# A fused two-block model on one core: the forgetting row in two parts, gates through a scratch row, c as one row, recurrence steps between tiles, one FFN product moved

## What is computed

```python
# first_block
mod = silu(c) @ w_ada + b_ada                    # c: 2048, w_ada: 2048 x 12288
sh1, sc1, gt1, sh2, sc2, gt2 = split(mod, 6)     # gt1, gt2: the two gates, rows of 2048
h = rmsnorm(x, g_mix) * (1 + sc1) + sh1
x = x + gt1 * hybrid_mixer(h, ...)
h = rmsnorm(x, g_ffn) * (1 + sc2) + sh2
x = x + gt2 * ((silu(dwconv(h @ w_gate)) * (h @ w_up)) @ w_down)

# forgetting attention, in the mixer, 8 heads
F = cumsum(log_sigmoid(f_logit + b_f))
s = q @ k.T * scale + F[t] - F[s]                # causal, softmax, @ v

# recurrence, in the mixer
log_a = -8 * gate_r * softplus(-lam);  a = exp(log_a)
inp = sqrt(-expm1(2 * log_a)) * (gate_i * xc)
h = scan(h = a * h + inp);   y_lru = h * gelu(yb)

# second block, twice; its last step
x = x + merged @ w_out
```

## Time and profile before

| | |
|---|---|
| median of 3 runs | 3060.62 us (3060.08 to 3062.21) |
| the profiled execution, its time | 3060.53 us |
| its span | 3058.7 us |
| granted TensorE clock, mean | 0.998 |
| busy: TensorE / its weight loads | 3026.9 us (99%) / 2543.3 (83%) |
| busy: DVE / ACT / POOL | 1973.8 (65%) / 1502.3 (49%) / 13.0 |
| read from HBM | 655 MB, 215 GB/s over the span |

### The profile page before, as it was taken

The page is one execution under the profiler, slowest core; times in us unless marked ns, Lnnn a source line. Parts: engine busy times, 40 slices in busy tenths (PEclk is TensorE's granted clock), DMA queues, the critical chain, the costliest instruction groups (busy, mean ns, idle before and its releaser), DMA issues.

```text
span 3058.7 us, 38978 instructions
## 1 busy us (share of the span) xinstructions
PE 3026.9 (99%) x14626; PEld 2543.3 (83%) x14626; DVE 1973.8 (65%) x2077; ACT 1502.3 (49%) x1804; POOL 13.0 (0%) x28
## 2 busy tenths in 40 slices
PE   7999999999999999999999999999999999999999
PEld 6899888888888888888888888888888888888887
DVE  7988887875666567675555656565475555556564
ACT  5555456544444445554444344544555454444543
POOL 0000000000000000000000000000000000000000
PEclk9999999999999999999999999999999999999999
DMA  9997887865555555455555445555455555445455
GB/s 400 416 383 290 338 343 278 315 244 193 190 186 190 188 185 179 165 179 179 193 172 193 166 170 193 173 186 186 160 183 175 194 175 194 166 167 193 168 183 191
DMA packets 167622, 659.24 MB, mean 216 GB/s; under 512 B 18592, under 2 KB 18880, under 8 KB 155200
## 3 DMA queue, kind: packets, MB, share of 16 engines
q1 hardware_dynamic: 164256, 637.99, 59.3%
q0 software_dynamic: 3232, 19.36, 1.7%
HBM read 655.18 MB, written 2.10 MB: 215 GB/s over the span
## 4 chain that ended last, share of the span: by engine, by line
PE 94%; DVE 4%; DMA 1%; ACT 1%; issue 0%; ACTq 0%
PE pg L1175 27%; PE pg L1177 27%; PE pg L1176 27%; PE pm L1210 1%; DVE R L1746 1%; PE pm L1238 1%; DMA w_raw<-w 1%; DVE w_lo L1802 1%; PE pm L1633 1%; PE pg L1264 1%; PE pg L1266 1%; PE pg L1265 1%; PE pm L1175 1%; PE pm L1177 1%; PE pm L1176 1%; PE pm L1527 0%
## 5 line engine op out<-in xcount | busy, mean ns | idle before, releaser
L1682 DVE TENSOR_TENSOR w_lo<-w_raw,w_hi 128x1024 fp32r<-128x1024 f32 x872 | 1066.0, 1225 | 961.3 <-ACT w_hi L607 957.2
L607 ACT ACTIVATE w_hi<-w_raw 128x1024 fp32r<-128x1024 f32 x872 | 925.0, 1061 | 1306.2 <-PE pg L1177 1299.2
L1175 PE MATMUL pg<-w_hi,hT_hi 128*128 128x512 f32 x2912 | 1146.7, 394 | 15.8 <-DVE w_lo L1802 15.5
L1177 PE MATMUL pg<-w_hi,hT_lo 128*128 128x512 f32 x2912 | 1135.4, 390 | 0.0
L1176 PE MATMUL pg<-w_lo,hT_hi 128*128 128x512 f32 x2912 | 1135.0, 390 | 0.0
L1175 PEld LDWEIGHTS pg<-w_hi,hT_hi 128*128 128x128 f32 x2912 | 547.8, 188 | 131.6 <-issue 14.5
L1177 PEld LDWEIGHTS pg<-w_hi,hT_lo 128*128 128x128 f32 x2912 | 547.4, 188 | 115.3
L1176 PEld LDWEIGHTS pg<-w_lo,hT_hi 128*128 128x128 f32 x2912 | 547.9, 188 | 110.0
L1175 PE MATMUL pg<-w_hi,y_parts 128*128 128x512 f32 x864 | 337.9, 391 | 2.3 <-issue 1.4
L1177 PE MATMUL pg<-w_hi,y_parts 128*128 128x512 f32 x864 | 336.4, 389 | 0.0
L1176 PE MATMUL pg<-w_lo,y_parts 128*128 128x512 f32 x864 | 336.2, 389 | 0.0
(11 more groups left out here) (302 smaller groups left out, 1953.5 us busy)
## 6 DMA issues: line engine op xcount, KB each, us to landing
w_raw<-w SPq DMA_DIRECT2D x1012, 512.0 KB, 4.1
R<-w_ada SPq DMA_DIRECT2D x59, 1024.0 KB, 9.2
x_rows<-w_ada SPq DMA_DIRECT2D x18, 1024.0 KB, 8.8
R<-w_ada POOLq DMA_DIRECT2D x11, 1024.0 KB, 7.7
R<-w SPq DMA_DIRECT2D x16, 512.0 KB, 11.2
R<-w_ada SPq DMA_DIRECT2D x10, 512.0 KB, 6.4
R<-mem_T SPq DMA_DIRECT2D x8, 512.0 KB, 10.0
x_rows<-x SPq DMA_DIRECT2D x4, 1024.0 KB, 14.8
```

What stands on the lines that cost most here:

```text
L607: act.activation(w_hi[:, g % RING, :, :].rearrange("p c n -> p (c n)"), raw[:, g % RING, :], ACT.Copy).then_inc(hi_done, 1)
L1175: pe.matmul(out, hi, w_hi[:, slot, c, :], start=start, stop=False)
L1177: return pe.matmul(out, lo, w_hi[:, slot, c, :], start=False, stop=stop)
L1682: tt(flat(w_lo[:, g % RING, :, :]), raw[:, g % RING, :], flat(w_hi[:, g % RING, :, :]).bitcast(F32), ALU.subtract).then_inc(lo_done, 1)
```

## The change

- **c.** SP loads c as one row, and `con`'s first part, ahead of everything. TensorE spreads the row over the partitions with four fp32 products of `ones` (one partition) with 512 columns, into four banks, ahead of tile 0. ACT applies SiLU as it evicts them, behind memory part 0 and tiles 0 and 1.
- **F.** A new tile `F_parts` in fp32r holds the rounded row in partitions 0 to 7 and the rest in 32 to 39; `F_pick` has ones in both places of a head. One fp32r product takes the place of the fp32 one. DVE makes both behind the scan, a memset is added.
- **Gates.** `gate_row` transposes 16 columns of `mod` into 16 rows on TensorE, ACT copies them to SBUF, POOL stores the 8 KB to a scratch row in HBM, waits for it, and loads it spread over 128 partitions (1 MB). Gate 1 in POOL's program stands ahead of the blocks of w_ada and behind the second attention; gate 2 behind these blocks and ahead of the late constants.
- **Recurrence.** On ACT tile 70 moves ahead of Tanh, the copy of F_t and tile 71 ahead of Square, tile 72 ahead of Identity; DVE's two products get a finer wait and one moves behind tile 73.
- **FFN.** In turns 0 and 1 `weigh_odd(5)` moves behind `down_out` 0 and 1. In the end the last product moves ahead of one tile.
- **End.** No tiles of zeros; the last 512 columns are added and stored in two halves.

```diff
         F_row = mv[:, 1, 1, 0:S]
+        F_parts = mv_r[:, 1, 1, S:2 * S]
+        F_pick = small_r[:, 0:NH * 2]
+        gate_rows = [mv[0:KD, 1, 0, 0:P], con[0:KD, 2 * P:3 * P]]
+        gates = [nc.dram_tensor(f"gate_rows{h}", (1, D), F32, kind="Internal").ap() for h in range(2)]
...
                 if g == 0:
+                    sp.dma_start(flat(c_rows)[0:1, :], t["c"].partition_broadcast(1)).then_inc(c_in, 16)
+                    sp.dma_start(con[:, 0:2 * P], t["con"][:, 0:2 * P]).then_inc(con_in, 16)
                     memory(0)
...
                     sp.dma_start(vec[:, :], t["vec"]).then_inc(vec_in, 16)
-                    sp.dma_start(con[:, 0:2 * P], t["con"][:, 0:2 * P]).then_inc(con_in, 16)
                 if g in (1, 3, 5):
                     memory((g + 1) // 2)
-                if g == 2:
-                    sp.dma_start(flat(c_rows), t["c"].partition_broadcast(P)).then_inc(c_in, 16)
...
                 tiles(group)
-            tiles(GROUPS, count=RING)
-            for n in range(NB):
+            for n in range(NB - 1):
                 sp.wait_ge(xb_ready, LAYERS * NB + n + 1)
...
                              ).then_inc(out_stored, 16)
-            sp.wait_ge(out_stored, 16 * NB)
+            for tb in range(TB):
+                sp.wait_ge(out_half, tb + 1)
+                sp.dma_start(t["out"][:, tb, (NB - 1) * NW:], x[:, tb, (NB - 1) * NW:]).then_inc(out_stored, 16)
+            sp.wait_ge(out_stored, 16 * (NB - 1 + TB))
...
             pool.dma_start(band, t["band"]).then_inc(band_in, 16)
+            def gate(h, dest):
+                pool.wait_ge(gate_sb, h + 1)
+                pool.dma_start(gates[h].rearrange("o (m p) -> (o m) p", p=P), gate_rows[h]).then_inc(gate_out, 16)
+                pool.wait_ge(gate_out, 16 * (h + 1))
+                pool.dma_start(dest, gates[h].partition_broadcast(P)).then_inc(gate_in, 16)
+            pool.wait_ge(y_ready, 2)
+            pool.wait_ge(lru_dve, 4)
+            gate(0, gate_1)
             for n in range(BY_SP, len(BLOCKS)):
...
                                    t["w_ada"][n][:, first:last]).then_inc(ffn_ada_in[at], 16)
-            pool.wait_ge(y_ready, 2)
+            gate(1, gate_b)
...
-            def broadcast(h, dest, bank):
-                act.wait_ge(bc_ready, h + 1)
-                at = (h % 2) * AH
-                for n in range(2):
-                    act.activation(dest[:, at + n * NW:at + (n + 1) * NW],
-                                   pm[bank + n][:, :], ACT.Copy).then_inc(bc_done, 1)
+            def gate_row(h):
+                act.wait_ge(gate_T, h + 1)
+                act.activation(gate_rows[h], pm[0][0:KD, 0:P], ACT.Copy).then_inc(gate_sb, 1)
...
                 upto(2 * p + 2)
-                if p == 1:
-                    act.wait_ge(c_in, 16)
-                    act.activation(flat(c_rows), flat(c_rows), ACT.Silu).then_inc(c_ready, 1)
+                if p == 0:
+                    for n in range(NB):
+                        act.wait_ge(c_ps, n + 1)
+                        i = act.activation(flat(c_rows)[:, n * NW:(n + 1) * NW], pm[n][:, :], ACT.Silu)
+                    i.then_inc(c_ready, 1)
...
             i.then_inc(lru_act, 1)
+            upto(71)
             for b in range(4):
...
             i.then_inc(lru_act, 1)
-            act.wait_ge(lru_act, 4)
-            act.activation(flat(GR), flat(Y_), ACT.Square).then_inc(lru_act, 1)
-            act.wait_ge(lru_act, 5)
-            act.activation(flat(GR), flat(GR), ACT.Identity, bias=1.0, scale=0.044715).then_inc(lru_act, 1)
             upto(72)
...
             act.activation(flat(F_t), pm[2][:, 0:TB * 8], ACT.Copy, scale=-1.0).then_inc(F_sb, 1)
+            act.wait_ge(lru_act, 4)
+            act.activation(flat(GR), flat(Y_), ACT.Square).then_inc(lru_act, 1)
+            upto(73)
+            act.wait_ge(lru_act, 5)
+            act.activation(flat(GR), flat(GR), ACT.Identity, bias=1.0, scale=0.044715).then_inc(lru_act, 1)
...
             take(g0 + 1, 1, flat(u_tok))
-            broadcast(2, gate_b, 0)
-            broadcast(3, gate_b, 2)
+            act.wait_ge(y_ready, 2)
+            gate_row(1)
...
-            def broadcast(h, bank):
-                first = (M_GATE1, M_GATE1 + 8, M_GATE2, M_GATE2 + 8)[h]
-                pe.wait_ge(ada_used, first + 8)
-                for m in range(8):
-                    i = pe.matmul(pm[bank + m // 4][:, m % 4 * P:(m % 4 + 1) * P],
-                                  mod[:, first + m:first + m + 1].to_broadcast([P, P]), ident, start=True, stop=True)
-                i.then_inc(bc_ready, 1)
+            def gate_row(h):
+                first = (M_GATE1, M_GATE2)[h]
+                pe.wait_ge(ada_used, first + KD)
+                pe.transpose(pm[0][0:KD, 0:P], mod[:, first:first + KD], ident).then_inc(gate_T, 1)
...
                         pe.matmul(out, Q1[occ][:, h, tb * P:(tb + 1) * P], K1[occ][:, h, :], start=True, stop=False)
-                        i = pe.matmul(out, ident[:, forget + h:forget + h + 1].to_broadcast([P, P]), F_row,
+                        i = pe.matmul(out, F_pick[:, forget + h:forget + h + 1].to_broadcast([P, P]), F_parts,
...
+            pe.wait_ge(c_in, 16)
+            pe.wait_ge(con_in, 16)
+            for n in range(NB):
+                pe.matmul(pm[n][:, :], ones[0:1, :], flat(c_rows)[0:1, n * NW:(n + 1) * NW], start=True, stop=True
+                          ).then_inc(c_ps, 1)
             upto(12)
             pe.wait_ge(rows_ready, 1)
-            pe.wait_ge(con_in, 16)
+            pe.wait_ge(c_ready, 1)
...
             pe.wait_ge(F_sb, 1)
+            pe.wait_ge(F_split, 1)
             attn_at(71, 0, Zv[0], "k0", 0)
...
             upto(86)
-            broadcast(0, 0)
+            gate_row(0)
             upto(91)
             pe.wait_ge(y_T_sb, 2)
-            pe.wait_ge(bc_done, 2)
+            pe.wait_ge(gate_sb, 1)
             attn_at(91, 1, Zv[1], "k1", 4)
...
             y_T(1, o1)
-            upto(106)
-            broadcast(1, 0)
...
             pe.wait_ge(aT_ready, j + 1)
-            broadcast(2, 0)
-            broadcast(3, 2)
+            gate_row(1)
             for n in range(NB):
...
                 if n == 0:
-                    pe.wait_ge(bc_done, 8)
+                    pe.wait_ge(gate_sb, 2)
...
                                    ).then_inc(F_ready, 1)
+            dve.wait_ge(F_ready, 1)
+            step(dve.tensor_copy(F_parts[0:8, :], F_row[0:8, :]))
+            step(tt(F_pick, ident[:, 0:8], ident[:, 32:40], ALU.add))
+            step.settle()
+            tt(F_parts[32:40, :], F_row[0:8, :], F_parts[0:8, :].bitcast(F32), ALU.subtract).then_inc(F_split, 1)
...
             step.settle()
-            dve.wait_ge(lru_act, 4)
+            dve.wait_ge(lru_act, 3)
             step(tt(flat(X_), flat(A_), flat(A_), ALU.mult))
...
             upto(73)
+            dve.wait_ge(lru_act, 4)
             stt(flat(TH), flat(X_), 1.0, flat(TH), ALU.add, ALU.mult).then_inc(lru_dve, 1)
+            upto(74)
...
                     split(g0 + 2, (i,))
-                    weigh_odd(i)
+                    if i < 5:
+                        weigh_odd(i)
                 down_out(g0 + 2, j, 0)
...
                 down_out(g0 + 2, j, 1)
+                weigh_odd(5)
...
             down_out(g0 + 2, j, 1)
-            split(g0 + 3, range(2))
-            dve.wait_ge(bc_done, 8)
+            split(g0 + 3, range(1))
             product(NFF - 1, aT2_hi, aT2_lo)
+            split(g0 + 3, range(1, 2))
...
                     dve.wait_ge(tile_used, tile0 + use.end)
+                    if l == LAYERS - 1 and use.n == NB - 1:
+                        for tb in range(TB):
+                            xs = x[:, tb, use.n * NW:]
+                            tt(xs, xs, pg[b][:, tb, :], ALU.add).then_inc(out_half, 1)
+                        return
...
                     while fed < t:
-                        split((tile0 + fed) // GT, (fed % GT,))
+                        if l < LAYERS - 1 or fed < LTILES:
+                            split((tile0 + fed) // GT, (fed % GT,))
```

More of the change, by code:

```diff
@@ L427, in build @@
         waited = sem("waited")
[L428 to L429 removed]
+        c_in, c_ps, c_ready, ada_used, gate_T, mod_taken, mod2_ready = map(
+            sem, ("c_in", "c_ps", "c_ready", "ada_used", "gate_T", "mod_taken", "mod2_ready"))
         hT_hi_done, hm_ready, xr_ready = map(sem, ("hT_hi_done", "hm_ready", "xr_ready"))
@@ L888, in _ @@
             upto(90)
-            broadcast(0, gate_1, 0)
+            gate_row(0)
             attn_at(96, 1, S1[1], PT1)
@@ L894, in _ @@
                 refill(6 + q, pm[2 + q][:, :].rearrange("p (c s) -> p c s", c=2))
-            upto(110)
-            broadcast(1, gate_1, 0)
             def block_squares_1(n):
@@ L1876, in _ @@
             step(dve.memset(F_row, 0.0))
+            step(dve.memset(F_parts.bitcast(F32), 0.0))
             for tb in range(TB):
```

17 lines of the change are left out of this document (10 added, 7 removed).

## The result

The changed kernel takes 3042.36 us (median of 4, 3041.05 to 3044.99) against 3060.35 us for the kernel before beside it; the ratio is 0.994, interval 0.9928 to 0.9952. Its profiled execution took 3042.21 us with a span of 3040.4. 3044.0 was predicted, 3039 to 3049.

The account below looks back on a forecast made before the run. TensorE, busy 99% of the span, was taken as the bound, with DMA saturated in early stages. Gains 2.2 + 6.3 + 3.2 + 1.0 + 1.5 + 2.3 = 16.5 us off 3060.5 gave 3044.0, range 3039.0 to 3049.0.

Parts of the forecast that it names:

- (1): Start: c as one row removes a 1024 KB load from the DMA-saturated first stage; 2.2 us gained, bounds -1 and 2.6.
- (2): Attention logits: F in two fp32r parts makes eight of 16 products faster, 2.5 us in each attention.
- (3): First attention: recurrence steps between tiles bring DVE's chain 3.7 us sooner; together with F in two parts still 3.7.
- (4): Gates: one transpose replaces each pair of broadcasts; 1.5 us gained at the first broadcast, 3.2 at the last two.
- (5): Middle: lead of 7.7 us meets saturated DMA, gate 1's load takes 2.6; 6.3 gained, bounds 3.7 and 9.7.
- B: Middle: DMA doesn't cap it, ACT's waits there are order; gain 9.7 us, time 3040.6; chance 0.18.
- A: The DMA ledger holds: 3044.0 us, by itself 3042 to 3046.5, with small TensorE waits for `w_lo`; chance 0.47.
- (6): FFN: weighings moved behind `down_out` 0 and 1 gain 1.0 us (twice 0.5), last product ahead of one tile 1.5.
- rival E: Near 1190 us: constants queued behind gate 2 land too late for `lvec`, making the kernel slower than before; chance 0.02.
- (7): End: no tile of zeros, last add and store in halves; 2.3 us gained, bounds 2.0 and 3.0.
- C: The start gives nothing: 3046.2 us, or 3047 with a loss of 1; chance 0.17.
- D: DVE's chain gains less than 3.7 us, or POOL's transfers disturb the FFN's stream: 3047 to 3050 us; chance 0.15.

Follow-up runs that it names:

- c_behind_tile: The changed kernel with c's row and the first constants issued behind the first memory part and tile 0: 3041.75 us, ratio 0.9936.
- both: The changed kernel with c's row and first constants issued behind tile 0, and one weighing of tiles 85 to 112 moved into 113 to 126: 3041.89 us.
- three doses: The changed kernel with gate 1's last load at 8 KB, 1 MB (as changed) or 2 MB: 3041.26, 3042.36 and 3043.95 us.
- ffn_order_before: The changed kernel with the FFN's three moves undone: 3049.42 us, ratio 0.9960 against the kernel before.

## Why the prediction was right, point by point

(1) c: 2.2 predicted, 1.7 measured (2.0 alone). ACT's load wait named for it ended at 35.42 us, not near 34: 0.6 sooner than before; two tiles later the lead is there (2.96 at tile 10), so a single load was a poor witness of a ledger. One of the signs of being wrong did come: the start shows longer waits, ACT's 6.04 us against 5.19 and TensorE's 2.45 (at 37.79) against 2.06. In sum they are shorter: behind tile 0 TensorE waits three times, 4.2 us, where it waited seven times, 6.9. Behind the longest of them the granted clock fell in both kernels, to 0.57 in 38 to 42 us here and to 0.60 in 44 to 48 us before. The 0.4 us for the later start of the big transfers is not shown by any run (c_behind_tile gave 0.5 back, both 0.1); the rest is within what executions differ by. The products took 7.16 us, the slow one of the two cases, and cost nothing, as argued.

(2) and (3): first attention 3.7 predicted, 4.1 measured. DVE's tile 70 came 246.62 - 241.13 = 5.5 us sooner, 1.7 of it from the start: 3.8. Its idle time is 4.23 us ("near 4"), and the logits take 253.78 - 249.41 = 4.4 us ("4.2"). TensorE's waits at the transposes are 0.88 and 0.72, where one of 1 to 1.5 was named. The step that failed is "this can gain 2.18 us and some tenths": what the kernel before lost at reduced clock, 1.7 us, came back too, so the recurrence alone gives 3.9. It mattered little for the sum, since DVE's lead was the limit I took: 0.4 us.

(4) First broadcast 1.66 (1.5), second attention 2.5 (2.5), late broadcasts 3.4 to 3.5 at tile 384 (3.2).

(5) The ledger: middle 6.8 measured, 6.3 predicted, and B's 9.7 did not come. The small waits for `w_lo` that A demanded are there, at a DMA share of 1.0. But the items were off in both directions, and that the middle came out within half a microsecond is in part luck. A megabyte was priced at 2.6 us of TensorE and cost about 1.3. Against that, 1.1 us were lost in the stretch without any load, and some tenths to 1.3 at the second attention's transposes (10.01 to 8.71), which were no item at all. "The 1.7 of the second broadcast is lost here" was right in size: 10.47 falls to 8.53. The Trainium skill, "DMA: Bandwidth & Descriptors", Rules for kernel authors, says that spreading transfers over the queues adds no bandwidth; by that rule a load on POOL's queue takes its time from SP's stream. The trace agrees: with gate 1's load among them the engines moved 398 GB/s in 350 to 390 us at a share of 1.01, no more than the 405 of SP's stream alone, and by the three doses TensorE felt about half of what the load needs.

(6) TensorE has no wait in the FFN, as said. Weighings: 0.8 each, 0.5 predicted; the waits themselves were 0.46 and 0.45, so what is lost around them was undersized. Product: 15.11 - 13.53 = 1.6 (1.5), right in size; but "a stretch in which nothing but TensorE is late" was wrong: ACT waits over 2 us for three tiles there, and in ffn_order_before TensorE for one of them. I had put the burst down as a danger to `lvec` alone (rival E) and left out the final norm's row (1 MB) and the tiles that go through the same engines.

(7) End: 3.2 (2.3, bounds 2.0 to 3.0), so outside its own bounds. The last store is issued 2.3 us sooner after TensorE's last product starts (3037.89 - 3036.15 = 1.7 against 4.0), near the 2.1 reckoned; the half-sized store, taken as 0.2, gave 0.9. That is the term that was mis-sized.

Rival E: `lvec` was read at 1181.55 us, without a wait. Issues on POOL, KB and median us to landing:

```profile
con_sb<-con POOLq DMA_DIRECT2D x1, 1344.0 KB, 11.7
small_w_sb<-small_w POOLq DMA_DIRECT2D x2, 576.0 KB, 8.3
...
lvec_sb<-lvec POOLq DMA_DIRECT2D x2, 14.0 KB, 8.7
```

For a transfer issued twice this is the middle of two. The `lvec` that is issued here, alone:

```profile
DMA to landing us min/median/max: 13.4/13.4/13.4
```

The constants, issued at 1159.81, landed at 1171.5; the small weights took 12.4 us from 1160.33, to 1172.7, and `lvec` 13.4 from 1160.85, to 1174.3, seven microseconds ahead of the read. E's 118 GB/s, taken from one transfer alone, is no rate of the queue: gate 2 (1.05 MB), the constants (1.38) and the small weights (0.6), 3.03 MB, were in 13.5 us after the gate's issue at 1159.26, some 225 GB/s beside SP's stream. The Trainium skill, same page, Anatomy of one DMA, had given an estimated 17 us from the store on; from 1155.48 to 1174.3 it is 18.8. So the size is about right, though not by the way assumed: the four loads were not one after another but under way together, beside SP's stream.

The sum came within 1.8 us because its misses were small: -0.5, +0.5, +0.6, +0.3, +0.9. Four of the five are gains beyond the forecast, so they did not cancel; only inside the middle did errors offset each other. C and D are out by the table, B by the doses.

## What to carry to other kernels

Where a stage is limited by DMA, remove bytes; delays of the compute engines' first tiles disappear in it. Don't price the bytes at their full transfer time: here a megabyte needed 2.6 us of DMA and cost TensorE about 1.3. A burst that is moved to where nothing waits for its own data can still hold up the tiles beside it: price it at the next load that has to land in the same microseconds, and keep the step that TensorE needs ahead of that load. Price edits of one stage together: here one of them turned from 1.5 into some 5 us beside the other.

## What the runs showed of the hardware

A wait of TensorE can cost more than itself: 2.2 us at 268.84 cost 3.9, with the clock at 0.54 behind it, and 2.77 us at 1181 were followed by 4 us at a granted clock of 0.50 and cost 5.7 with it, while the 1.39 us at 1191.61 in the kernel before cost little more than themselves. Four fp32 products of 512 columns from a single partition ahead of everything took 7.16 us, 1.79 each, and tile 0's products behind them came at 0.43 us, against 0.23 at the full clock; the profile's granted clock says 1.00 for these first microseconds all the same, so at the start of a trace the distances have to be read. Behind a last store of 256 KB the span ended 2.5 us after its issue, behind one of 512 KB after 3.4 and 3.5.
